# Projections of a two-block transformer in split fp32: high weights against both activation halves in one 512-column pass

## The reference, cut to what matters

```
x = x + mix @ w_out[l]                                     # end of every mixer (4 of them)
hf = rms_norm(x, ffn_norm[l]) @ w_up[l]                    # first kind of feed-forward (2 of them)
gate, val = hf[..., :D_FF], hf[..., D_FF:]
gate = depthwise_conv(gate, conv_w[l], conv_b[l])
x = x + (gelu(gate) * val) @ w_down[l]
...
x = x + 0.5 * (silu(h @ w_gate) * (h @ w_up)) @ w_down      # second kind of feed-forward (4 of them)
```

## Time and profile before

| | |
|---|---|
| median of 3 runs | 1890.3 us (1887.63 to 1890.84) |
| span of the profiled execution | 1882.6 us |
| around the span, against the median | 7.7 us |
| mean granted clock of TensorE | 0.942 |
| PE busy | 1712.7 us (91%) |
| weight loads (PEld) busy | 1625.1 us (86%) |
| DVE busy | 1230.0 us (65%) |
| ACT busy | 860.1 us (46%) |
| POOL busy | 495.1 us (26%) |

### The profile page before, as it was taken

One profiled execution on the slowest core, in us unless ns is written; L12 is line 12 of the kernel. 1 busy time (PEld: TensorE's weight loads), 2 busy tenths in 40 slices (PEclk: granted clock), 3 DMA queues, 4 the chain that ended last, 5 costly groups with the idle time before them and its releaser, 6 DMA issues. The chain is left out here.

```text
span 1882.6 us, 35550 instructions
## 1 busy us (share of the span) xinstructions
PE 1712.7 (91%) x13260; PEld 1625.1 (86%) x13260; DVE 1230.0 (65%) x1750; ACT 860.1 (46%) x1250; POOL 495.1 (26%) x511
## 2 busy tenths in 40 slices
PE   5887799999977999999999456999999999789999
PEld 5775799998856999999999435999999998579999
DVE  7677666657786766655557986655555556865553
ACT  3445355533543555444444243544354434435442
POOL 3040333310211433223320002333123311343320
PEclk9987899999986999999999757999999999899999
DMA  6330256644320556656654301566455654235563
GB/s 223 101 112 23 90 170 178 222 161 135 102 67 23 159 179 194 198 164 179 196 200 135 101 1 56 177 182 215 164 168 180 212 179 145 67 101 179 179 214 99
DMA packets 70800, 274.25 MB, mean 146 GB/s; under 512 B 7872, under 2 KB 9024, under 8 KB 70592
## 3 DMA queue, kind: packets, MB, share of 16 engines
q1 hardware_dynamic: 70272, 271.04, 46.3%
q0 software_dynamic: 448, 2.13, 0.3%
HBM read 272.09 MB, written 1.05 MB: 145 GB/s over the span
## 5 line engine op out<-in xcount | busy, mean ns | idle before, releaser
L744 DVE TENSOR_TENSOR wl<-raw,wh 128x1024 fp32r<-128x1024 f32 (+1 forms) x474 | 632.5, 1335 | 299.5 <-ACT wh L504 298.7
L1130 PE MATMUL gb<-hh,wh 128*128 128x256 f32 x2768 | 802.4, 290 | 26.3 <-DVE wl L744 17.0
L1131 PE MATMUL gb<-hl,wh 128*128 128x256 f32 x2768 | 788.6, 285 | 0.0
L1132 PE MATMUL gb<-hh,wl 128*128 128x256 f32 x2768 | 787.9, 285 | 0.0
L504 ACT ACTIVATE wh<-raw 128x1024 fp32r<-128x1024 f32 (+1 forms) x474 | 528.5, 1118 | 343.7 <-PE gb L1132 339.6
L1130 PEld LDWEIGHTS gb<-hh,wh 128*128 128x128 f32 x2768 | 536.6, 194 | 41.6 <-DVE wl L744 17.0
L1131 PEld LDWEIGHTS gb<-hl,wh 128*128 128x128 f32 x2768 | 536.9, 194 | 3.2 <-issue 2.9
L1132 PEld LDWEIGHTS gb<-hh,wl 128*128 128x128 f32 x2768 | 536.6, 194 | 0.0
L1131 PE MATMUL gb<-gul,wh 128*128 128x256 f32 x1056 | 298.7, 283 | 0.0
L1132 PE MATMUL gb<-guh,wl 128*128 128x256 f32 x1056 | 298.3, 282 | 0.0
L1130 PE MATMUL gb<-guh,wh 128*128 128x256 f32 x1056 | 296.5, 281 | 1.8 <-POOL gul L493 1.7
(11 more groups left out here) (190 smaller groups left out, 1666.5 us busy)
## 6 DMA issues: line engine op xcount, KB each, us to landing
raw<-in_wa SPq DMA_DIRECT2D x378, 512.0 KB, 3.6
raw<-in_wb SPq DMA_DIRECT2D x96, 704.0 KB, 4.1
x<-in_x SPq DMA_DIRECT2D x1, 1024.0 KB, 4.9
out_x<-x SPq DMA_DIRECT2D x8, 128.0 KB, 3.1
row<-in_row POOLq DMA_DIRECT2D x1, 836.0 KB, 10.6
tab<-in_bias SPq DMA_DIRECT2D x3, 256.0 KB, 4.4
con<-in_const POOLq DMA_DIRECT2D x1, 544.0 KB, 7.7
tab<-in_bias SPq DMA_DIRECT2D x1, 512.0 KB, 4.8
```

The costliest lines, as they stand in the source:

```text
L744: nc.vector.tensor_tensor(wl[:, slot, 0:nt * P], raw[:, slot, 0:nt * P], wh[:, slot, 0:nt * P].bitcast(f32), ALU.subtract).then_inc(s_lo, 1)
L1130: nc.tensor.matmul(bank, a, rhs_h(k), start=start and k == 0, stop=False)
L1131: nc.tensor.matmul(bank, a, rhs_l(k), start=False, stop=False)
L1132: last = nc.tensor.matmul(bank, b, rhs_h(k), start=False, stop=stop and k == nt - 1)
```

## The change

Activation pairs are laid out side by side (`hx`, `mx`, `gux`, each with two planes; `hh`, `hl` and so on are views of them), so that one matmul can take both as a moving operand of 2 x 256 columns. A new helper `joined` replaces `tiles` for: all up units of ffn2 (the first unit too), the value units of ffn1, all down units, all out units of mixers. The gate units of ffn1, the input units of mixers stay with `tiles`. The high-activation sum lies in the first half of the bank, the sum of `wh` with the low activations in the second; both must be added:

- in ffn2, gate: ACT copies the second half to `low` (in `ptb`), DVE adds the first half to it, DVE multiplies by `rstd` (before: one multiplication from PSUM);
- in both kinds, value: ACT copies the second half, DVE adds the first half into `gu`, DVE multiplies by `tap` in place (before: one multiplication from PSUM);
- chunks of x: two additions instead of one, with a wait between them.

```
+            def joined(i, slot, bank, nt, both, high, start, stop, ready=None):
+                pe.wait_ge(s_lo, i + 1)
+                for k in range(nt):
+                    if ready is not None:
+                        ready(k)
+                    a, b = wh[:, slot, k * P:(k + 1) * P], wl[:, slot, k * P:(k + 1) * P]
+                    if k < nt - 1:
+                        nc.tensor.matmul(bank[:, :], a, both(k), start=start and k == 0, stop=False)
+                        nc.tensor.matmul(bank[:, 0:SEQ], b, high(k), start=False, stop=False)
+                    else:
+                        nc.tensor.matmul(bank[:, 0:SEQ], b, high(k), start=False, stop=False)
+                        last = nc.tensor.matmul(bank[:, :], a, both(k), start=False, stop=stop)
+                last.then_inc(s_pe, 1)
...
 ACT, up:
+                    if not conv:
+                        act.wait_ge(s_pe, i + 1)
+                        nc.scalar.activation(low[:, j, 0, :], gb[2 * j][:, SEQ:2 * SEQ], ACT.Copy).then_inc(s_gl, 1)
+                        ahead(0)
                     act.wait_ge(s_gs, p + 1)
...
-                    ahead(0)
                     if conv:
+                        ahead(0)
                         act.wait_ge(s_conv, it * 2 + (C + j + 1))
                         nc.scalar.activation(tap[:, j, :], tap[:, j, :], ACT.Gelu).then_inc(s_gelu, 1)
+                    act.wait_ge(s_pe, i + 2)
+                    nc.scalar.activation(low[:, j, 1, :], gb[2 * j + 1][:, SEQ:2 * SEQ], ACT.Copy).then_inc(s_vl, 1)
                     ahead(1)
...
 DVE, up:
                     if not conv:
+                        dve.wait_ge(s_gl, it * 2 + (B0[n] + j + 1))
+                        nc.vector.tensor_tensor(gate, gb[2 * j][:, 0:SEQ], low[:, j, 0, :], ALU.add).then_inc(s_gadd, 1)
+                        dve.wait_ge(s_gadd, it * 2 + (B0[n] + j + 1))
+                        nc.vector.tensor_tensor(gate, gate, rstd[:, :], ALU.mult).then_inc(s_gs, 1)
                         ahead(0)
...
-                    dve.wait_ge(s_up, p + 1)
-                    dve.wait_ge(s_pe, i + 2)
                     if not isinstance(p, int) or p >= 2:
                         dve.wait_ge(s_gul, p - 1)
-                    nc.vector.tensor_tensor(gu[:, j, :], val[:, 0:SEQ], t, ALU.mult).then_inc(s_gu, 1)
+                    dve.wait_ge(s_vl, p + 1)
+                    nc.vector.tensor_tensor(gu[:, j, :], val[:, 0:SEQ], low[:, j, 1, :], ALU.add).then_inc(s_vadd, 1)
+                    dve.wait_ge(s_up, p + 1)
+                    dve.wait_ge(s_vadd, p + 1)
+                    nc.vector.tensor_tensor(gu[:, j, :], gu[:, j, :], t, ALU.mult).then_inc(s_gu, 1)
                     ahead(1)
...
 DVE, out units (down chunks alike, with scalar_tensor_tensor):
-                    nc.vector.tensor_tensor(xc, gb[o % 4][:, 0:SEQ], xc, ALU.add).then_inc(s_xo, 1)
+                    nc.vector.tensor_tensor(xc, gb[o % 4][:, 0:SEQ], xc, ALU.add).then_inc(s_xa, 1)
+                    dve.wait_ge(s_xa, DC * n + o + 1)
+                    nc.vector.tensor_tensor(xc, gb[o % 4][:, SEQ:2 * SEQ], xc, ALU.add).then_inc(s_xo, 1)
```

More of the change, by code:

```diff
@@ L112, in build_program @@
     G0 = [FC * sum(k == "ffn1" for k, _ in PHASES[:n]) for n in range(NPH)]
+    B0 = [FC * sum(k == "ffn2" for k, _ in PHASES[:n]) for n in range(NPH)]
     Y0 = [sum(IN_UNITS.get(k, 0) for k, _ in PHASES[:n]) for n in range(NPH)]
@@ L130, in build_program @@
         x = sb("x", [P, DC * SEQ])
[L131 to L134, removed]
+        hx = sb("hx", [P, 2, DC * SEQ], r32)
+        hh, hl = hx[:, 0, :], hx[:, 1, :]
+        mx = sb("mx", [P, 2, DC * SEQ], r32)
+        mh, ml = mx[:, 0, :], mx[:, 1, :]
         prm = sb("prm", [P, NPRM])
@@ L151, in build_program @@
         with ExitStack() as turn:
-            guh = sb("guh", [P, FC * SEQ], r32, turn)
-            gul = sb("gul", [P, FC * SEQ], r32, turn)
+            gux = sb("gux", [P, 2, FC * SEQ], r32, turn)
+        guh, gul = gux[:, 0, :], gux[:, 1, :]
         y = sb("y", [P, 26 * SEQ])
@@ L1091, in down @@
                     nc.vector.scalar_tensor_tensor(out=xc, in0=gb[j][:, 0:SEQ], scalar=1.0 if conv else 0.5, in1=xc,
+                                                   op0=ALU.mult, op1=ALU.add).then_inc(s_xa, 1)
+                    dve.wait_ge(s_xa, it * 2 + (DC * n + j + 1))
+                    nc.vector.scalar_tensor_tensor(out=xc, in0=gb[j][:, SEQ:2 * SEQ], scalar=1.0 if conv else 0.5, in1=xc,
                                                    op0=ALU.mult, op1=ALU.add).then_inc(s_xo, 1)
@@ L1145, in first_unit, with ready @@
                     pe.wait_ge(s_xo, DC * n - 1)
-                tiles(i, i % RING, gb[0][:, 0:SEQ], DC, lambda k: mc(hh, k), lambda k: mc(hl, k), True, True,
-                      lambda k: pe.wait_ge(s_hl, DC * n + k + 1))
+                def ready(k):
+                    pe.wait_ge(s_hl, DC * n + k + 1)
+                if PHASES[n][0] == "ffn2":
+                    joined(i, i % RING, gb[0], DC, both_h, lambda k: mc(hh, k), True, True, ready)
+                else:
+                    tiles(i, i % RING, gb[0][:, 0:SEQ], DC, lambda k: mc(hh, k), lambda k: mc(hl, k), True, True, ready)
                 norm(n)
@@ L1329, in mixer @@
                         pe.wait_ge(s_xo, DC * n + o - 3)
-                    tiles(i, i % RING, gb[o % 4][:, 0:SEQ], DC, lambda k: mc(mh, k), lambda k: mc(ml, k), True, True)
+                    joined(i, i % RING, gb[o % 4], DC, lambda k: view(mc(mh, k), [[DC * SEQ, 2], [1, SEQ]]),
+                           lambda k: mc(mh, k), True, True)
             def feed_forward(n, kind, l):
@@ L1343, in up @@
                             pe.wait_ge(s_gu, it * 2 + (F + j - 1))
-                        tiles(i, (U + 2 * j + k) % RING, gb[2 * j + k][:, 0:SEQ], DC, lambda k: mc(hh, k), lambda k: mc(hl, k),
-                              True, True)
+                        slot, bank = (U + 2 * j + k) % RING, gb[2 * j + k]
+                        if kind == "ffn1" and k == 0:
+                            tiles(i, slot, bank[:, 0:SEQ], DC, lambda c: mc(hh, c), lambda c: mc(hl, c), True, True)
+                        else:
+                            joined(i, slot, bank, DC, both_h, lambda c: mc(hh, c), True, True)
                 for j in range(2):
@@ L1357, in down @@
                             pe.wait_ge(s_xo, it * 2 + (DC * n + j - 1))
[L1358 to L1361, removed]
+                        joined(it * 4 + b, b % RING, gb[j], KD,
+                               lambda c: view(mc(guh, k * KD + c), [[FC * SEQ, 2], [1, SEQ]]),
+                               lambda c: mc(guh, k * KD + c), k == 0, k == 1,
+                               (lambda c: pe.wait_ge(s_gul, F + k * KD + c + 1)) if first and j == 0 else None)
                 pe.wait_ge(s_gu, F + FC - 1)
```

11 lines of the change are left out of this document (8 added, 3 removed).

## The result

The changed kernel takes 1864.8 us (median of 4 runs, 1862.3 to 1866.7), the one before 1889.0 (4 runs, 1884.7 to 1890.8): a ratio of 0.987 (0.9857 to 0.9882), 24 us off. Forecast were 1836 us, 54 off. The range held it, and it came out at rival (b), 1864. The profiled execution took 1864.96 us, its span is 1863.2.

A forecast was written before the change was run, and what follows sets the result against it. PE was taken as the bound in ffn2 and the down units, DVE in ffn1's up units and out units. -58.9 + 4.0 + 0.3 + 0.5 = -54.1 us gave 1836 us; range 1812 to 1867.

The forecast's parts named there:

- (b): Rival, 15%: the 13 ns are paid per pass, whatever its width; 31.3 us off, 4.8 back, 1864 us.
- What bounds the kernel: PE binds ffn2 and the down units; DVE's loop binds ffn1's up units; DVE is nearly full in out units.
- What a k-tile costs after: Where PE binds: 215 ns for 512 columns plus 120 for 256, 335 instead of 360; 58.9 us saved together.
- The additions: Extra DVE sums: 4.0 us lost in out units, 0.3 between phases, 0.5 before the last store; none in ffn1.
- ffn1: Up units: value passes get shorter but PE waits longer for DVE's loop; 0 gained, 0 lost.
- The cover for the addition: In ffn1's up units the value addition of 0.42 us stands in DVE's 0.81 us wait for POOL; cost 0.
- Between phases: After feed-forward phases x's last chunk comes 0.46 us later, mostly covered by 0.58 us; 0.3 us lost before ffn2.
- The 7.7 us between span and median: Whole kernel: 7.7 us added to the forecast span of 1828.5 us to give 1836 us.
- (a): Rival, 15%: the load is no limit, a 256-column pass takes 111 ns; 80.1 us off, 4.8 back, 1815 us.
- (d): Rival, 9%: a joined pass takes 240 ns, no k-tile gets shorter and the 4.8 us of additions stay; 1895 us.
- (c): Rival, 8%: the forecast holds but ffn1's loop takes the addition, 20 us; 1856 us.

The follow-up runs named there:

- the plain order: Changed kernel with the last k-tile of a joined unit kept in the others' order (512 columns, then 256) instead of turned: 1856.1 us, ratio 0.9833.

## Why the prediction was wrong, point by point

**What bounds the kernel** was right: PE, at the upper clock, with no idle time in ffn2 and the down units, before and after.

**What a k-tile costs after** is the step that failed: "I take 215 ns for the pass of 512 columns". It moved the behaviour of fp32 passes (425 ns, "nothing on top") to fp32r passes, and gave the 13 ns at 256 columns to the pair of load and pass. Passes alone show 13.3 to 14.0 ns on top at 256, 320, 384 and 512 columns. The two rows could not separate a cost per pass from a load that takes its turn, since all fp32r passes in that trace were 256 wide; the one wide row was of another type. What can go is one pass's 13 ns, and the mix of two widths takes back up to 7 of them: 8 to 9 ns in the kernel where 25 were taken. Over 2356 k-tiles that is the 20.6 us of the first two rows of the table, not 58.9. This term alone is off by 38 us, the whole forecast by 29; the other terms gave back some.

The section "Back-to-back issue gap" of the Trainium skill's "TensorE: Matmul & The Clock Gate", whose 262 and 518 cycles the prediction turned into 109 and 216 ns, agrees with bf16 passes here (107.5 and about 216) and not with fp32r ones (120 and 227).

**The additions** (+4.8 forecast) cost nothing, as three passes with all of them ran no longer than the kernel before. In ffn2 DVE stayed under PE as worked out. In the out units the sum was made with DVE's old busy time of 20.1 us plus 3.7; but the old time held splits stretched to 1.65 us, and after the change all but the first take 1.23. I take it that they meet POOL's products at other moments; that was not tried apart.

**ffn1** (0 forecast) gained 5.0 us. The cover for the addition was right (0.81 us of idle time became 0.30). Three things were missed. The loop of 5.88 us had 0.17 us in it that were neither DVE's work nor POOL's but sequencer instructions behind the late wait; the changed kernel has none there. PE waits for the loop only in the last 17 or 18 of the 44 units before; in the first ones it has a lead and takes 2.88 us for each. The window that I read was late in the phase. And with the loop at 5.71 us the joined value units do count: with three passes and all else changed, ffn1's up units took 256.7 us, with joined ones 254.1.

**Between phases:** the sum of squares is fetched at 1358.09, 0.07 us after POOL ends it (1357.19 + 0.83), at the very end of the first unit; the row is in the profile's timeline:
```profile
1357.19 0.83 POOL L414 TENSOR_TENSOR acc<-acc,sq 128x256 f32<-128x256 f32 x1
...
1358.09 0.68 PE L1175 MATMUL mb<-acc,con 128*128 128x256 f32 x2
```
That cover of 0.58 us is used up, as forecast. Nothing is bare here: the pass before it, at 1357.86, is one of 512 columns, and PE comes 0.23 us behind it, as behind any other.

**The 7.7 us between span and median** were taken for time around the span. They are not: after the change 1.8 us lie around it (1864.96 against 1863.2). The profiled execution before thus took some 1884.4 us, well below the median, and so did the fourth run of that kernel with 1884.7.

**Rivals.** (b) was right in mechanism, but for what the mix of widths takes back, and, by luck of two errors, to 1 us: 31.3 off and 4.8 back were 20.6 off and some 4 more gained elsewhere. (a) and (d) are refuted by the bare passes (120 at 256, 227 at 512), (c) by the loop, which got shorter. With nothing that told them apart in the trace, 50% for one reading against 15% for (b) was too sure.

## What to carry to other kernels

Ask of a price per instruction whether it belongs to the columns, the load or the pass, and don't carry it from one type to another; where every row has the same width, the trace can't tell, and both readings deserve a like chance. Joining passes saves the fixed part of one pass, here 13 ns of 360, and mixing widths can take half of that back, so try the plain order before a clever one. In a loop, look at how far behind its release an instruction starts and at what the sequencer does in between, and read a loop over its whole phase, not in one window.

## What the hardware showed that I had not expected

- An fp32r pass at 2.4 GHz takes its columns plus 13.3 to 14.0 ns (120.0 at 256, 146.7 at 320, 173.8 at 384, 227 at 512), with no other engine at work and with all of them at work on SBUF alike. Only 448 columns took more, 202.9, which is 16.2 on top. A bf16 pass of 256 took 107.5.
- Passes of 512 and 256 columns in turn run at 353.3 or at 346.7 ns a pair, from the same addresses, by what ran before them, and either goes on by itself. Twenty-four bf16 passes moved it from slow to fast, groups of eight back to slow; one fp32r pass of 128 columns moved nothing.
- A narrower weight load shortens a 256-column pass (113.4 ns with 32 columns) and lengthens a 512-column one (229.9 with 96, against 227).
- Inside a hardware loop on DVE two register instructions of the sequencer stood between a late wait and the product behind it, which began 0.21 us after its release; outside the loop, with the late wait ahead of a met one as well, 0.04. With one sequencer instruction between them it was 0.11, with none, and the late wait on the product itself, 0.04.
